# A two-layer trunk with seven-product feed-forwards: sums of squares on VectorE, two early conversions, paired weight loads in down

## The reference, cut to what matters

```python
D_MODEL, D_FF = 1024, 2816
def rms_norm(x, g):
    return x * lax.rsqrt(jnp.mean(x * x, -1, keepdims=True) + EPS) * g
def swiglu(h, w_gu, w_d):
    gu = h @ w_gu
    return (jax.nn.silu(gu[..., :D_FF]) * gu[..., D_FF:]) @ w_d
hp = hp + yp                                  # output projection of the mixer
hp = hp + swiglu(rms_norm(hp, norm_ffn[layer]), w_gate_up[layer], w_down[layer])
```

## Time and profile before

| | before |
|---|---|
| median of three runs | 1317.92 us |
| the profiled execution: its own time | 1320.59 us |
| its span, first to last instruction | 1319.1 us |
| TensorE busy | 1220.4 us (93%) |
| VectorE busy | 1051.2 us (80%) |
| ScalarE busy | 684.6 us (52%) |
| GpSimd busy | 359.2 us (27%) |
| mean granted TensorE clock | 0.982 |
| DMA | 193.37 MB, 126230 packets, mean 147 GB/s |

### The profile page before, as it was taken

How to read it: one execution, slowest core, us unless ns; L and a number is a source line. 1 busy time by engine, 2 the same in 40 slices (tenths; PEclk the granted TensorE clock), 3 DMA queues, 4 the chain that set the end, 5 groups by cost and what they waited for, 6 DMA issues and landing times. The chain is left out here.

```text
span 1319.1 us, 26917 instructions
## 1 busy us (share of the span) xinstructions
PE 1220.4 (93%) x10559; PEld 1007.2 (76%) x10559; DVE 1051.2 (80%) x1741; ACT 684.6 (52%) x1179; POOL 359.2 (27%) x571
## 2 busy tenths in 40 slices
PE   9999997899999888899999999999779999998997
PEld 7767686687787777778888888887667787787786
DVE  5446667799999977677877878876669999999785
ACT  6243554565555544336554565654555465554443
POOL 2004322000001124247455555553310010011320
PEclk9999998899999999999999999999889999999999
DMA  8658555676767599430123232132556776766982
GB/s 270 208 190 279 149 160 125 163 189 164 202 172 161 129 223 219 85 113 34 37 93 97 65 97 71 60 96 85 156 148 167 182 189 164 202 142 131 207 164 75
DMA packets 126230, 193.37 MB, mean 147 GB/s; under 512 B 7801, under 2 KB 88953, under 8 KB 121882
## 3 DMA queue, kind: packets, MB, share of 16 engines
q1 hardware_dynamic: 96730, 157.06, 38.1%
q0 software_dynamic: 29376, 34.61, 17.9%
HBM read 180.53 MB, written 11.11 MB: 145 GB/s over the span
## 5 line engine op out<-in xcount | busy, mean ns | idle before, releaser
L2516 PE MATMUL P<-arena,wh 128*128 128x260 f16 x2288 | 396.7, 278 | 67.3 <-DVE arena L1748 30.8
L2516 PE MATMUL P<-arena,wl 128*128 128x260 f16 x1144 | 317.6, 278 | 0.0
L2516 PEld LDWEIGHTS P<-arena,wh 128*128 128x128 f16 x2288 | 222.3, 99 | 116.0 <-issue 46.3
L1037 ACT ACTIVATE wh<-arena 128x1024 f16<-128x1024 f32 (+2 forms) x138 | 123.1, 896 | 142.9 <-PE P L2516 94.2
L2516 PE MATMUL P<-zh,wh 128*128 128x260 f16 x704 | 194.2, 276 | 3.0 <-DVE wl L1729 3.0
L2516 PE MATMUL P<-zh,wl 128*128 128x260 f16 x704 | 193.2, 274 | 0.0
L2516 PE MATMUL P<-zl,wh 128*128 128x260 f16 x704 | 193.0, 274 | 0.0
L1729 DVE SCALAR_TENSOR_TENSOR wl<-arena,wh 128x1024 f16<-128x1024 f32 (+2 forms) x138 | 145.3, 1053 | 46.6 <-ACT wh L1037 45.9
L1729 DVE SCALAR_TENSOR_TENSOR wl<-stage,wh 128x1024 f16<-128x1024 f32 (+2 forms) x116 | 132.5, 1143 | 11.8 <-ACT wh L1037 11.2
L1037 ACT ACTIVATE wh<-stage 128x1024 f16<-128x1024 f32 (+2 forms) x116 | 114.0, 984 | 27.3 <-PE P L2516 25.1
L2516 PEld LDWEIGHTS P<-arena,wl 128*128 128x128 f16 x1144 | 112.6, 98 | 18.6
(11 more groups left out here) (422 smaller groups left out, 2650.5 us busy)
## 6 DMA issues: line engine op xcount, KB each, us to landing
arena<-w_gu SPq DMA_DIRECT2D x56, 512.0 KB, 6.0
stage<-w_in SPq DMA_DIRECT2D x23, 1024.0 KB, 5.6
stage<-w_gu SPq DMA_DIRECT2D x44, 512.0 KB, 5.2
...
```

The source lines that it names most:

```text
L1037: nc.scalar.activation(ringh[:, o:o + block_words(n)], source(kind, n), ACT.Copy, scale=WS).then_inc(c_hi, 1)
L2516: mm = nc.tensor.matmul(bank, w[:, o:o + 128], x[:, k, :], start=(i in (0, 1, 3) and k == a and w is ringh and x is xh), stop=(k == z - 1 ...
```

## The change

Four things. The running sums of squares (`square_in`) go from GpSimd to VectorE, at places in VectorE's own order. The conversions of B11(0) and T3(0) both stand, on ScalarE, right behind the weighing of tile 5, ahead of its high parts and square; on VectorE both low parts follow the operand sums of tile 5. From unit 13 on (`NS = NG + 2`) one transfer with rows of 256 words per step brings two blocks, B11 with B21 or B12 with B22, and T3 and T1 become sums on VectorE. SyncE's order changes: T3(1) is loaded ahead of the wait for the squares, the small loads stand partly ahead of B11(13), and the rest and the next weights behind all down loads. Of the rest of the diff, which adapts counts and waits, parts are left out.

```diff
+NS = NG + 2
...
+        A3P = [arena[:, AS_AT + 1536 * i:AS_AT + 1536 * i + 1536] for i in range(2)]
+        Z4P = [arena[:, ZX_AT + 1536 * i:ZX_AT + 1536 * i + 1536] for i in range(2)]
...
-                s = {"B11": Z4[p], "B12": Z4[2 + p], "B22": E2[p], "B21": A4[1], "T3": A4[2 + p], "T2": A4[0]}[kind]
+                w = block_words(n)
+                if kind in ("T3", "T2"):
+                    return E2[kind == "T3"][:, 0:w].rearrange("p (k c) -> p k c", c=128)
+                pair = (A3P if kind in ("B11", "B21") else Z4P)[p][:, 0:2 * w]
+                return pair.rearrange("p (k two c) -> p two k c", two=2, c=128)[:, int(kind in ("B21", "B22"))]
+            if kind == "B21" and n == 12:
+                s = S5[3]
...
             def ffn_load(kind, n, layer):
+                if n >= NS:
+                    a, z = k_range(n)
+                    j, dst = (0, A3P) if kind == "B11" else (1, Z4P)
+                    sp.dma_start(dst[n % 2][:, 0:2 * block_words(n)],
+                                 w_dn[layer][2 * ((n - NG) // 2) + j][:, 256 * a:256 * z]
+                                 ).then_inc((ld1, ld2)[j][n % 2], 16)
+                    return
...
                 ffn_load("B11", 1, layer)
+                sp.wait_ge(c_lo, base + 2)
+                ffn_load("T3", 1, layer)
                 sp.wait_ge(ssq_ready, KD * (1, 3)[layer])
                 ffn_load("B22", 1, layer)
-                for n in range(2, NU):
-                    if n in (13, 14):
-                        sp.wait_ge(f_mm, PRODUCTS * layer + 14 * NG)
-                    sp.wait_ge(c_lo, base + 7 * (n - 2) + 2)
-                    ffn_load("T3", n if n > 14 else n - 1, layer)
+                for n in range(2, NS):
+                    if n > 2:
+                        sp.wait_ge(c_lo, base + 7 * (n - 2) + 2)
+                        ffn_load("T3", n - 1, layer)
                     sp.wait_ge(c_lo, base + 7 * (n - 2) + 5)
-                    if n == 14:
-                        ffn_load("T3", n, layer)
                     ffn_load("B11", n, layer)
                     ffn_load("T1", n, layer)
-                    sp.wait_ge(c_lo, base + 7 * (n - 2) + (7 if n == 14 else 6))
+                    sp.wait_ge(c_lo, base + 7 * (n - 2) + 6)
                     ffn_load("B21", n - 1, layer)
                     sp.wait_ge(c_lo, base + 7 * (n - 2) + 7)
                     ffn_load("B22", n, layer)
-                    if n == 14 and layer == 0:
-                        sp.wait_ge(f_lo, NG)
-                        sp.dma_start(wabf, wab.rearrange("p k n -> p (k n)")).then_inc(l1_in, 16)
-                        sp.dma_start(gate[0:8, 0:2], gates).then_inc(l1_in, 16)
-                        sp.dma_start(cw, convw).then_inc(l1_in, 16)
-                        sp.dma_start(msk, masks).then_inc(l1_in, 16)
-                        sp.dma_start(cext, conv_state).then_inc(l1_in, 16)
-                        sp.dma_start(dS[0], delta_state[0]).then_inc(st_in[0], 16)
-                    if n == 16 and layer == 0:
-                        for u in range(2):
-                            weights(w_in1, FIRST_UNIT["in1"] + u, u, u, WORDS[FIRST_UNIT["in1"] + u])
-                sp.wait_ge(c_lo, base + 7 * (NU - 2) + 6)
-                ffn_load("B21", NU - 1, layer)
+                sp.wait_ge(c_lo, base + 7 * (NS - 2) + 2)
+                ffn_load("T3", NS - 1, layer)
+                sp.wait_ge(c_lo, base + 7 * (NS - 2) + 4)
+                ffn_load("B21", NS - 1, layer)
+                sp.wait_ge(f_mm, PRODUCTS * layer + 14 * NG)
+                sp.wait_ge(c_lo, base + 7 * (NS - 2) + 7)
+                ffn_load("B12", NS, layer)
+                if layer == 0:
+                    sp.wait_ge(f_lo, NG)
+                    sp.dma_start(wabf, wab.rearrange("p k n -> p (k n)")).then_inc(l1_in, 16)
+                    sp.dma_start(gate[0:8, 0:2], gates).then_inc(l1_in, 16)
+                    sp.dma_start(cw, convw).then_inc(l1_in, 16)
+                sp.wait_ge(c_lo, base + 7 * (NS - 1) + 2)
+                ffn_load("B11", NS, layer)
+                sp.wait_ge(c_lo, base + 7 * (NS - 1) + 7)
+                ffn_load("B11", NS + 1, layer)
+                ffn_load("B12", NS + 1, layer)
+                for n in range(NS + 2, NU):
+                    sp.wait_ge(c_lo, base + 7 * (n - 2) + 6)
+                    ffn_load("B11", n, layer)
+                    sp.wait_ge(c_lo, base + 7 * (n - 2) + 7)
+                    ffn_load("B12", n, layer)
+                if layer == 0:
+                    for u in range(2):
+                        weights(w_in1, FIRST_UNIT["in1"] + u, u, u, WORDS[FIRST_UNIT["in1"] + u])
+                    sp.dma_start(msk, masks).then_inc(l1_in, 16)
+                    sp.dma_start(cext, conv_state).then_inc(l1_in, 16)
+                    sp.dma_start(dS[0], delta_state[0]).then_inc(st_in[0], 16)
...
             def second_term(kind, n, layer):
-                if n >= NU:
+                if n >= NS:
                     return
...
@@ -734,22 +762,14 @@
                 b = (1, 3)[layer]
                 if layer == 1:
                     pool.wait_ge(outs, 16 * 7)
-                for k in range(KD):
-                    square_in(b, k)
-                    if k in (3, 4, 6):
-                        second_term("T3" if k == 3 else "T1", int(k == 6), layer)
+                for kind, n in (("T3", 0), ("T1", 0), ("T1", 1)):
+                    second_term(kind, n, layer)
                 for n in range(NU):
                     second_term("T3", n + 1, layer)
                     second_term("T1", n + 2, layer)
-                    if n in (13, 15, 17):
-                        for k in (n - 13, n - 12):
-                            square_in(b + 1, k)
                     if layer == 0 and n in (14, 15, 16):
                         block_masks(2 * (n - 14))
                         block_masks(2 * (n - 14) + 1)
-                if layer == 0:
-                    for k in (6, 7):
-                        square_in(b + 1, k)
...
-                if kind == "B11":
+                if kind == "B11" or kind == "B21" and n >= NS:
                     act.wait_ge(ld1[p], first_load(p, n, layer))
...
@@ -1239,6 +1257,10 @@
                     act.wait_ge(outs, 16 * 7)
                 for at in range(KD):
                     weigh(layer, at)
+                    if at == 5:
+                        act.wait_ge(mm_done, FIRST_TILE[name] + 6)
+                        convert(0, layer)
+                        convert(1, layer)
                     if at == KD - 1:
...
-                    if at == 5:
-                        act.wait_ge(mm_done, FIRST_TILE[name] + 6)
-                        convert(0, layer)
-                    if at == 6:
-                        convert(1, layer)
...
+            def square_in(b, k):
+                dve.wait_ge(sq_ready, KD * b + k + 1)
+                if k == 0:
+                    dve.wait_ge(stat_ready, b)
+                    ins = nc.vector.tensor_copy(ssq[:, :], sq[:, 0, :])
+                else:
+                    dve.wait_ge(ssq_ready, KD * (b - 1) + k)
+                    ins = nc.vector.tensor_tensor(ssq[:, :], ssq[:, :], sq[:, k % 2, :], ADD)
+                ins.then_inc(ssq_ready, 1)
...
+                base, p = NB7 * layer, n % 2
+                if kind == "T3":
+                    dve.wait_ge(ld2[p], first_load(p, n, layer))
+                    dve.wait_ge(c_lo, base + 7 * (n - 1) + (4 if n == NS else 2))
+                    a, b = source("B12", n), source("B22", n)
+                elif kind == "T1":
+                    dve.wait_ge(ld1[p], first_load(p, n, layer))
+                    dve.wait_ge(t_sum, len(SUMS) * layer + SUM_AT["T3", n])
+                    a, b = source("B12", n), source("B11", n)
+                elif kind == "T2":
+                    if n < NS:
+                        dve.wait_ge(t1_sum, 16 * (NS * layer + n + 1))
+                        dve.wait_ge(ld2[p], first_load(p, n, layer))
...
+                        dve.wait_ge(t_sum, len(SUMS) * layer + SUM_AT["T1", n])
...
                 nc.vector.tensor_tensor(source(kind, n), a, b, ADD).then_inc(t_sum, 1)
...
                 low_part(m, layer)
                 if i == 2:
                     weight_sum("T4", n, layer)
-                if i == (6 if n == 12 else 5):
+                if n + 1 >= NS:
+                    if 4 <= i:
+                        weight_sum(("T3", "T1", "T2")[i - 4], n + 1, layer)
+                elif i == 5:
                     weight_sum("T2", n + 1, layer)
...
+                        if n in (13, 15, 17) and i in (4, 6):
+                            square_in(b + 1, n - 13 + (i == 6))
...
                     leave_tile(name, at, FFN_ROWS[layer][at], at % 2)
                     if at >= 1:
                         operand_lows(layer, at - 1)
+                        square_in((1, 3)[layer], at - 1)
...
                     if at == 5:
```

(5 more changed lines are left out.)

56 lines of the change are left out of this document (24 added, 32 removed).

## The result

| | before | changed |
|---|---|---|
| median | 1318.22 us (4 runs, 1317.85 to 1321.44) | 1297.01 us (4 runs, 1295.71 to 1298.52) |
| the profiled execution: its own time | 1320.59 us | 1297.56 us |
| VectorE busy | 80% | 82% |
| GpSimd busy | 27% | 22% |
| mean granted TensorE clock | 0.982 | 0.986 |

The account below looks back on a forecast made before the run. TensorE was taken as busy in 93% of the span, leaving only its stops to win; -5.2 - 3.3 + 1.4 + 2.0 - 11.3 - 3.5 = -19.9 us took the median from 1317.92 to 1298.0 us, range 1291 to 1310.

Parts of the forecast that it names:

- Start of the first feed-forward: First layer, up to T3(1)'s gate: earlier conversions, leave of tile 7 and loads let TensorE run on 5.2 us earlier.
- the collision with GpSimd: First feed-forward's start: GpSimd's add no longer stretches line 1697 on VectorE, -1.1 us.
- the whole 1.9 us that 0.5 MB costs: First start's accumulating DMA: full saving from 0.5 MB less on its queues, used only for the 6.5 us bound.
- Start of the second: Second layer's feed-forward start: tile 7 leaves 3.1 us earlier, adds cost 1.0, DMAs give 0.9 and 0.3: -3.3 us.
- Unit 12: Down, unit 12: three sums on VectorE and, in the first layer, late B11(13) lengthen stops: +2.0 first layer, +1.4 second.
- Units 13 to 18: First layer's down: 12.1 us of stops and 1.2 of clock go, 2.0 of stops behind VectorE come: -11.3 us.
- Second layer's down: 2.79 us of stops and 1.5 of clock go, 0.8 of stops behind VectorE come: -3.5 us.
- Nothing between: GpSimd's other adds, those before the second mixer and at the end, cost nothing: 0 us.
- VectorE as the bound of down (1): Down: each product costs VectorE another 0.2 us of waiting, giving 1307 us; chance 0.16.
- The start's DMAs do not follow (2): Both starts: T3(1) lands only with the whole load backlog, 1.5 us gained instead of 8.5, 1305 us; chance 0.11.
- Pairs not early (3): Down: blocks of 14 to 18 land as late as now, only the start gains, 1311 us; chance 0.06.
- strided operands dear (4): Down: VectorE operations reading every other 128 words take 0.6 us more each, +46 us, 1344 us; chance 0.07.

Follow-up runs that it names:

- run 1: The change with the sums of squares, adds of down included, back on GpSimd, all else kept: 1297.37 us.
- run 3: The change with T3(1) loaded behind B22(1) as before, all else kept: 1299.71 us.
- Run 4: The change's pairs and load order in down alone, with squares, conversions and T3(1)'s load as in the kernel before: 1307.69 us.
- run 5: The change measured again, 1297.87 us, and the change with the load of B11(13)/B21(13) ahead of the wait for `f_lo`, 1296.08 us.
- run 8: The kernel before with only the masks, states and first two units of w_in1 loaded behind all first-layer down loads: 1308.48 us.
- run 9: The change with the state, mask and w_in1 loads back between the down loads: 1296.71 us.
- run 10: The change with each pair transfer cut into two transfers of rows of 128 words, sums still on VectorE: 1299.03 us.
- the second measurement: The whole change timed and profiled once more, without any edit: 1297.87 us.
- run 6: The change with T3(1) summed on VectorE as B12(1) + B22(1) in place of the accumulating DMA, in each layer: 1285.12 us.

## Why the prediction was right, and where it was not

**The median, 1298.0 against 1297.01 us**, is nearer than its terms deserve, and that is luck: by stretches, the two starts gave 4.1 us more than forecast and the first layer's down 2.1 more, the second layer's down 2.0 less and the mixer's start 1.6 less; and 1.8 of the 23.1 us between the two profiles are only how far each lay above its median.

- *Start of the first feed-forward, -5.2:* it was -6.96, beyond the bound of -6.5. The mechanism is the forecast one. Mis-sized were the collision with GpSimd, which I charged once (-1.1) and which stretched several instructions on both sides (the leave came 5.8 earlier, not 4.7; run 1 puts 0.8 of it on the squares, net of their adds, where I had them at nothing (-1.1 + 1.2)), and the loads: with T3(1) out of the chain the wait was 1.67 us shorter, where I had taken -0.9 and kept "the whole 1.9 us that 0.5 MB costs" as a bound. Run 3 returns it to 5.56 us.
- *Start of the second, -3.3:* -5.6, beyond the bound of -4.5. Counted from the weight split's stop, the leave of tile 7 came 4.4 us earlier (3.1 forecast). Of that, 1.2 us are there at the leave of tile 6 already and are the clock, not the change: in the two stretches of 4 us behind that stop it was 0.50 and 0.87 before, 0.67 and 1.00 in the change. Run 4, which has this projection as before, had 0.64 and 1.00 and its leave of tile 7 1.1 us earlier. From tile 6 to tile 7 the change gave 3.2 us, as forecast. The term that was too small is B22(1)'s landing, 1.9 in place of 0.9. With 0.85 us lost between leave and load and 0.2 behind the landing this is 5.2 us at the gate; the last 0.4 us is one stop of 1.55 us in gate and up of before that is 1.20 now.
- *Unit 12, +2.0 and +1.4:* the stops are 0.99 + 1.76 us, against 0.50 (at the end of unit 11) and 2.14 before, and 0.67 + 0.39 against 0.52 in the second layer: +0.1 and +0.5. The 3.6 us that I had forecast for unit 12 of the first layer are 2.75, in two stops, and the fall of the clock that I had put at 0.5 us did not come (1.00 in the 4 us behind the second). The wait for B11(13) behind `f_lo` is there, 1.19 us where I had 2.6, and run 5 takes it away for 1.3 us. The load was issued at 457.67, as forecast after the shift of 7 us; VectorE wanted it 0.7 us later than I had thought and the pair landed in some 4.4 us, not 4.8.
- *Units 13 to 18, -11.3:* about -11.5. Stops of 1.6 us are left, 2.0 forecast, and most lie where they were forecast, in the products with a leave, a low part and a sum. But the reason that I gave joins causes that are not all needed: run 8 shows that moving 3.4 MB of other loads alone returns 8.8 us of it, run 9 that with pairs and sums these loads are free, run 10 that the row length has no part that can be measured. I also wrote that a third of the traffic was read twice; of a unit's seven blocks, three were (13 MB by the two pages). VectorE was busy for 90% there, not above 95.
- *Second layer's down, -3.5, with +1.4 for its unit 12:* -0.1 in this profile and -1.3 in the second measurement (107.44 us), where I had -2.1. The stop of 2.79 us is gone. Two things stand against it. One is the clock, by which the two measurements of the change differ: behind the 3.2 us stop at the head it was 0.50 for 4 us and 0.75 for the next 4, against 0.62 and 1.00, and before it was 0.65 and 1.00. The other is the change itself: the adds of squares on VectorE cost 1.2 us here (run 1), while I had 0.8 us for all stops behind VectorE. The first 8 us behind that head, the change, then the kernel of run 3:

```profile
1178.71:1182.71 4.00, 4.00 (x19) 2.83 (x20) 3.87 (x6) 0.00 (x0) 0.00 (x0) 0.50 0.00 0
1182.71:1186.71 4.00, 4.00 (x29) 3.10 (x28) 3.03 (x8) 1.62 (x3) 0.00 (x0) 0.75 0.62 201
```
```profile
1182.38:1186.38 4.00, 4.00 (x36) 3.38 (x36) 3.87 (x6) 0.74 (x1) 0.00 (x0) 1.00 0.00 0
1186.38:1190.38 4.00, 3.03 (x28) 2.55 (x27) 3.55 (x8) 2.19 (x4) 0.00 (x0) 1.00 0.59 201
```

  At 1.00 throughout, run 3 takes 107.44 us like the second measurement at 0.62: TensorE then gets ahead and stops 0.97 and 0.73 us for VectorE. Only the longer fall, to 0.50 and 0.75, cost 1.2 us. I had no term for the clock behind this head.
- *Nothing between, 0:* +1.6 at the second mixer's start, by the clock (0.79 in its first 8 us against 1.00 before; run 3, with the change's code there, had 1.00 and took 39.20 us), and -0.6 before the weight split, whose stop is 5.68 in place of 6.29 us (6.28 again in run 1).

**The rivals.** VectorE as the bound of down (1): only in small, stops of 0.26 to 0.54 us there. The advice of the Trainium skill, page "Perfetto Trace Analysis", section "Optimizing Scalar/DVE Operations", to unload a busy VectorE, which I had set beside it, would here be run 1: 1.2 us gained in the second layer's down, and nothing in sum. The start's DMAs do not follow (2): they did, more than forecast. Pairs not early (3) and strided operands dear (4): no DMA wait is left behind unit 12, and the sums and low parts kept 0.96 us away from the masks.

**The largest miss is one of aim.** I wrote that TensorE "still stops there for some 4 us" at the gate of T3(1), and took it as given. Run 6 shows that it held 12.8 us in both layers together: the change shortened the way to that gate by 7 us and left the 10.6 us of the accumulating DMA as they were, beside a VectorE that waited 6.8 us for it.
